# RWKV chunks: block-inverse matrices as 32x32 diagonal blocks, their products in 32x32 tiles

## The reference, cut to what matters

```
def wkv7_scan(r, w, k, v, a, b):
    def step(state, inp):
        r_t, w_t, k_t, v_t, a_t, b_t = inp
        sa = jnp.einsum('bhvk,bhk->bhv', state, a_t)
        state = state * w_t[:, :, None, :] + sa[..., None] * b_t[:, :, None, :] + v_t[..., None] * k_t[:, :, None, :]
        y_t = jnp.einsum('bhvk,bhk->bhv', state, r_t)
        return state, y_t
...
    g = jax.nn.sigmoid(xg @ g1) @ g2          # g1: 1024 x 160, g2: 160 x 1024
...
    y = wkv7_scan(r_h, decay, k_h, v_h, -kk, kk * a_h)   # 16 heads of 64
...
    return (y * g) @ w_o
```

## Time and profile before

| what | us |
|---|---|
| median of 3 runs (1687.45, 1694.29, 1691.63) | 1691.63 |
| the profiled execution, whole | 1687.7 |
| its span, first to last instruction | 1685.9 |
| PE busy in it | 1653.5 |
| stage of the change: chunks, 1368.2 to 1462.7 | 94.5 |
| gate, first part (L1190, L1192), from 1331.8 | 7.1 |
| gate, second part (L1207, L1208), from 1361.2 | 7.0 |

### The profile page before, as it was taken

One profiled execution on the slowest core, in us unless ns is written; L12 is line 12 of the kernel. 1 busy time (PEld: TensorE's weight loads), 2 busy tenths in 40 slices (PEclk: granted clock), 3 DMA queues, 4 the chain that ended last, 5 costly groups with the idle time before them and its releaser, 6 DMA issues.

```text
span 1685.9 us, 32004 instructions
## 1 busy us (share of the span) xinstructions
PE 1653.5 (98%) x11846; PEld 1456.5 (86%) x11846; DVE 1081.1 (64%) x1979; ACT 947.3 (56%) x1416; POOL 1126.6 (67%) x505
## 2 busy tenths in 40 slices
PE   8999999999999999999999999999999999999998
PEld 6888889999999999888888769888888899888887
DVE  5324242997546766679999986455557975855555
ACT  5458553445544444566555667565667942356555
POOL 6964776788788898776676438656476551846463
PEclk9999999999999999999999999999999999999999
DMA  8544444566655455689999945555543412155551
GB/s 309 197 150 145 155 150 175 163 193 194 187 169 169 154 170 156 189 306 366 377 374 403 411 182 176 199 201 190 184 162 121 168 27 78 53 197 181 197 187 74
DMA packets 95998, 330.35 MB, mean 196 GB/s; under 512 B 32896, under 2 KB 33424, under 8 KB 78368
## 3 DMA queue, kind: packets, MB, share of 16 engines
q1 hardware_dynamic: 84448, 295.32, 51.3%
q0 software_dynamic: 11312, 33.68, 5.2%
q10 hardware_dynamic: 144, 0.07, 0.0%
HBM read 322.73 MB, written 5.24 MB: 195 GB/s over the span
## 4 chain that ended last, share of the span: by engine, by line
PE 74%; POOL 10%; issue 6%; DVE 4%; DMA 3%; ACT 3%; POOLq 0%; DVEq 0%; SPq 0%; ACTq 0%
PE bank L1088 8%; POOL rows_lo L3096 7%; PE bank L893 7%; PE bank L1109 6%; PE bank L968 5%; PE bank L899 4%; PE bank L1092 4%; PE bank L636 4%; PE bank L642 4%; PE bank L637 4%; PE bank L1224 3%; PE bank L925 3%; PE bank L959 2%; PE bank L963 2%; PE bank L965 2%
## 5 line engine op out<-in xcount | busy, mean ns | idle before, releaser
L3081 POOL TENSOR_TENSOR unit_lo<-unit_raw,unit_hi 128x2048 fp32r<-128x2048 f32 (+1 forms) x86 | 336.1, 3926 | 145.2 <-ACT unit_hi L1697 118.9
L3096 POOL TENSOR_TENSOR rows_lo<-rows_raw,rows_hi 128x1024 fp32r<-128x1024 f32 x128 | 309.2, 2417 | 73.1 <-ACT rows_hi L1817 46.0
L3171 POOL TENSOR_TENSOR up_lo<-up_raw,up_hi 128x2048 fp32r<-128x2048 f32 x22 | 111.3, 5057 | 156.6 <-ACT up_hi L1977 127.0
L1895 ACT ACTIVATE rows_hi<-rows_raw 128x1024 fp32r<-128x1024 f32 x128 | 135.8, 1061 | 118.1 <-PE bank L968 111.3
L2657 DVE TENSOR_TENSOR rows_lo<-rows_raw,rows_hi 128x1024 fp32r<-128x1024 f32 x128 | 160.3, 1256 | 23.3 <-ACT rows_hi L1895 23.0
L1697 ACT ACTIVATE unit_hi<-unit_raw 128x2048 fp32r<-128x2048 f32 x70 | 134.0, 1919 | 65.5 <-PE bank L642 36.8
L1088 PE MATMUL bank<-x_lo_hi,up_hi 128*128 128x512 f32 x640 | 159.8, 392 | 0.1
L899 PE MATMUL bank<-x_lo_hi,rows_lo 128*128 128x256 f32 x1024 | 143.3, 283 | 0.5 <-POOL rows_lo L3096 0.5
L899 PEld LDWEIGHTS bank<-x_lo_hi,rows_lo 128*128 128x128 f32 x1024 | 135.7, 190 | 6.4 <-POOL rows_lo L3096 0.9
L3134 POOL DMA_INDIRECT gathered<-in_v,picked_row x64 | 91.7, 1433 | 71.2 <-DVE bank L2647 61.5
L1088 PEld LDWEIGHTS bank<-x_lo_hi,up_hi 128*128 128x128 f32 x640 | 116.2, 189 | 21.9 <-issue 0.3
(11 more groups left out here) (511 smaller groups left out, 4186.3 us busy)
## 6 DMA issues: line engine op xcount, KB each, us to landing
unit_raw<-in_ring SPq DMA_DIRECT2D x70, 1024.0 KB, 4.9
rows_raw<-in_u SPq DMA_DIRECT2D x128, 512.0 KB, 3.6
rows_raw<-in_v SPq DMA_DIRECT2D x128, 512.0 KB, 7.2
up_raw<-in_up SPq DMA_DIRECT2D x44, 1024.0 KB, 5.0
down_raw<-in_down SPq DMA_DIRECT2D x22, 1024.0 KB, 5.0
unit_raw<-in_ring SPq DMA_DIRECT2D x20, 256.0 KB, 3.6
kept_hidden<-table SPq DMA_DIRECT2D x16, 256.0 KB, 4.1
const<-in_const SPq DMA_DIRECT2D x1, 1792.0 KB, 14.2
```

The costliest lines, as they stand in the source:

```text
L1895: A(rows_hi[q % 2][:, :], rows_raw[q][:, :], ACT.Copy).then_inc(S("v_hi_ready"), 1)
L3081: return nc.gpsimd.tensor_tensor(unit_lo[SLOT_OF[n]][:, w], unit_raw[SLOT_OF[n]][:, w], hi, ALU.subtract)
L3096: nc.gpsimd.tensor_tensor(rows_lo[q][:, :], rows_raw[q][:, :], rows_hi_f[q % 2], ALU.subtract).then_inc(S("u_lo_ready"), 1)
L3171: nc.gpsimd.tensor_tensor(whole(up_lo[l][s][1]), whole(up_raw[l][s][1]), as_f32(up_hi[s][1]), ALU.subtract).then_inc(S("up_lo1_ready"), 1)
```

## The change

The matrices of the inverse are block diagonal at 32 for most of the steps. They are now kept as their four 32x32 diagonal blocks (two heads of two blocks) in 256 columns in place of 512, and a product of two such matrices is a `block_products`: for each of the eight pairs four matmuls of 32x32 by 32x32, in four tiles of the array. That is 32 calls in place of 16. Eight products per chunk take this form (`x2`, `x4`, `r2`, `y8`, `r3`, `r4`, `mT`, `w`). The last two (`nT`, `tt`), which fill the lower left corner, have two tiles and 16 calls as before.

- DVE: the turns and sums of these matrices have 256 columns; a new add packs the masked matrix (`m_xd`), `corners` copies the corner blocks into `m_inv`.
- ACT: the copies have 256 columns; for the last chunk two activations write the diagonal blocks of `m_inv`.
- POOL: `first_sum` and `across_split` have 256 columns, `halves_placed` (512 columns) writes the diagonal blocks of `m_inv` for the first three chunks; six small steps at its start.
- Gate: the odd ranks are made in two column tiles of 128 tokens each (16 calls of 128 columns in place of 8 of 256); in the second part 16 calls of 128 columns for the first 128 ranks and 16 calls for the odd ranks with 32 rows each, at partitions 0 and 64, in place of 8 and 8 of 256 columns. `GATE2` is loaded by three DMAs in place of one.
- The stage begins when `rT` is scaled; `kfT` and the copy `dec_end` follow. SP waits for `halves_placed` before it loads `WO`.

```diff
+            def block_products(name, lhs, rhs, tiles=((0, 0), (1, 1), (2, 2), (3, 3))):
+
+                o = fill(name, len(tiles))
+                ends = [None] * len(tiles)
+                for p in range(PAIRS):
+                    for i, (k, m) in enumerate(tiles):
+                        ends[i] = mm(o[quarter(m), p * BLK:(p + 1) * BLK], lhs(quarter(k), p), rhs(quarter(k), p), start=True, stop=True)
+                full_by_heads(name, ends)
...
             def fourths(c, e):
                 made(c, "x2")
                 wait_turned("x2", c)
-                products(("x4", c), by_pair(m_y2[e]), by_pair(m_x2[e]))
+                block_products(("x4", c), by_pair(m_y2[e]), by_pair(m_x2[e]))
                 pe.wait_ge(S("r1_ready"), c + 1)
-                products(("r2", c), by_pair(m_y2[e]), inv_of(c))
+                block_products(("r2", c), by_pair(m_y2[e]), by_pair(m_iv[e]))
...
             def within_64(c, e):
                 wait_turned("q32", c)
-                products(("nT", c), by_pair(m_ex[e]), by_pair(m_x2[e]))
+                block_products(("nT", c), corner_of(e), by_pair(m_x2[e]), ((0, 1), (2, 3)))
...
             for k in range(KT):
-                t = mm(o[0:32, SEQ:2 * SEQ], g1[:, k * 160 + 128:(k + 1) * 160], mx_gate[:, k, :], start=k == 0, stop=k == KT - 1)
+                for c in range(TC):
+                    ends[c] = mm(o[last_ranks(c), SEQ:SEQ + P], g1[:, k * 160 + 128:(k + 1) * 160], mx_gate[:, k, c * P:(c + 1) * P], start=k == 0, stop=k == KT - 1)
...
-            for b in range(4):
-                o = fill(("g2", b))
-                for m in range(2):
-                    at_ = (2 * b + m) * P
-                    mm(o[:, m * SEQ:(m + 1) * SEQ], g2[:, at_:at_ + P], lora[:, 2, :], start=True, stop=False)
-                    t = mm(o[:, m * SEQ:(m + 1) * SEQ], g2[:, 1024 + at_:1024 + at_ + P], lora[:, 3, :], start=False, stop=True)
+            for b in range(2):
+                outs = [fill(("g2", c, b)) for c in range(TC)]
+                for m in range(4):
+                    at_ = (4 * b + m) * P
+                    for c in range(TC):
+                        mm(outs[c][:, m * P:(m + 1) * P], g2[:, at_:at_ + P], lora[:, 2, c * P:(c + 1) * P], start=m == 0, stop=False, skip_group_check=True)
+                for m in range(4):
+                    at_ = 1024 + (4 * b + m) * P
+                    for c in range(TC):
+                        r = last_ranks(c)
+                        t = mm(outs[c][:, m * P:(m + 1) * P], g2[r, at_:at_ + P], lora[r, 3, 0:P], start=False, stop=m == 3, skip_group_check=True)
...
+            def halves_placed(c):
+
+                wait_drained(g, ("w", c))
+                both = m_inv[c][:, :, :].rearrange("p m (n v) -> p m n v", n=2)
+                TT(both, bc(m_iv[c % 3][:, :, :].unsqueeze(2), [PAIRS, 2, BLK]), bc(own_half[:, :, :].unsqueeze(1), [PAIRS, 2, BLK]), ALU.mult).then_inc(S("halves_placed"), 1)
...
             for c in first:
                 x_of_chunk(c)
+            pe.wait_ge(S("chunks_ready"), 2)
             by_token(0)
-            for c in first:
+            squares(0, 0)
+            by_token(1)
+            for c in first[1:]:
                 squares(c, c)
-            by_token(1)
```

More of the change, by code:

```diff
@@ L426, in wait_loaded @@
         same = [m for m in range(n + 1) if SLOT_OF[m] == SLOT_OF[n]]
[L427 removed]
+        eng.wait_ge(raw_loaded[SLOT_OF[n]], 16 * sum(2 if m in (UNIT_AT["LORA1"], UNIT_AT["LORA2"]) else 3 if m == UNIT_AT["GATE2"] else 4 if m >= UNIT_AT["WO"] else 1 for m in same))
     def wait_released(eng, n):
@@ L2113, in _ @@
                 t = A(bonusT[:, m, :], bonusT[:, m, :], ACT.Copy, scale=col("r_k", m))
-            t.then_inc(S("bonus_scaled"), 1)
-            for b in range(4):
-                copy(("g2", b), gT[:, 2 * b:2 * b + 2, :])
+            t.then_inc(S("scaled_columns"), 1)
+            for b in range(2):
+                for c in range(TC):
+                    o = wait_filled(act, ("g2", c, b))
+                    drain(("g2", c, b), A(gT[:, 4 * b:4 * b + 4, c * P:(c + 1) * P], o[:, :].rearrange("p (m t) -> p m t", m=4), ACT.Copy))
             first = range(3)
@@ L2167, in _ @@
             rows_deviation(0)
-            copies(last, "nT", of(m_x4))
+            wait_drained(act, ("w", NRC - 1))
+            for n in range(2):
+                t = A(m_inv[NRC - 1][:, :, BLK * n:BLK * n + BLK], m_iv[lane(NRC - 1)][:, :, :], ACT.Copy, scale=own_half[:, n, 0:1])
+                step.mark(t) if n == 0 else t.then_inc(S("halves_placed"), 1)
+            block_copies(last, "nT", m_x4)
             wait_filled(act, ("ds", 1))
@@ L2964, in summed, with corners @@
                     wait_drained(ve, (after, c))
-                r = m_inv[c][:, :, :]
-                drain((name, c), V.tensor_tensor(r, eight(o), r, ALU.add))
+                r = m_iv[lane(c)][:, :, :]
+                drain((name, c), V.tensor_tensor(r, of_blocks(o), r, ALU.add))
+            def corners(c):
+                o = of_blocks(wait_filled(ve, ("tt", c)))
+                ve.wait_ge(S("halves_placed"), c + 1)
+                for par in range(2):
+                    r = quarter(2 * par)
+                    t = V.tensor_copy(m_inv[c][r, :, BLK:DK], o[r, :, :])
+                    step.mark(t) if par == 0 else drain(("tt", c), t)
             ve.wait_ge(S("compact_ready"), len(compact))
@@ L3034, in yg_lo_of @@
                     drain(("yt", th, b), V.tensor_tensor(yg_lo[w], o, yg_hi[w].bitcast(F32), ALU.subtract))
-            for b in range(4):
-                wait_drained(ve, ("g2", b))
+            for b in range(2):
+                for half in range(TC):
+                    wait_drained(ve, ("g2", half, b))
             o = eight(wait_filled(ve, ("y_", c)))
@@ L3211, in _ @@
                 step(nc.gpsimd.memset(eu16_c[DK * par:DK * par + half, half:DK], 0.0))
+            step(TT(ident_c[:, 0:BLK], ident_c[:, 0:BLK], ident_c[:, BLK:DK], ALU.add))
+            step(nc.gpsimd.memset(own_half[:, :, :], 0.0))
+            for n in range(4):
+                step(nc.gpsimd.memset(own_half[quarter(n), n % 2, :], 1.0))
             step(nc.gpsimd.memset(starts[:, :], 1.0))
@@ L3260, in _ @@
                 across_split(c)
+            for c in range(NRC - 1):
+                halves_placed(c)
             for c in (1, 2):
```

142 lines of the change are left out of this document (82 added, 60 removed).

## The result

The changed kernel takes **1718.62 us** (median of 5 runs, 1715.47 to 1720.3) against 1691.63 (median of 5 runs beside it, 1687.45 to 1696.07): ratio 1.0157, 95% interval 1.0142 to 1.0172. It is slower by 27.0 us, inside the predicted range and 8.6 us above the predicted 1710.

The account below looks back on a forecast made before the run. PE was taken to be bound by instruction arrival, about 3.75 us per 256. 18.3 + 5.5 - 3.2 - 1.0 = +19.6 us on a mean of 1690.3 gave 1710; own range 1700 to 1720, 8-in-10 range 1690 to 1726.

Parts of the forecast that it names:

- The first step: Dense part: PE already works at about the rate its instructions arrive, about 3.75 us per 256, as a limit, not a coincidence.
- First three chunks: Chunk stage's first part: 1536 more records, 16.0 blocks at 3.75 us, 61.3 us in all, an increase of 18.3 us.
- The 1.3 us for wide products at the start: Start of the chunks: three `x` products stand together and outlast their instructions' arrival; 1.3 us of 2.4 added.
- Bonus sums and first product of the last chunk: The stretch between the third chunk and the last chunk's later products; no change was forecast, 0.
- the rival of the fallen clock: Chunk stage: PE waiting for instructions with four small tiles looks idle, so the granted clock falls as well; 1722, chance 0.12.
- Last chunk: 1418.02 to 1442.70: 512 more records, 7.5 blocks, 30.2 us, so +5.5 us; the rest of the stage 0.
- The gate: Odd ranks in two tiles: -1.75 us in the first part, -1.65 in the second; -3.2 taken, bounds -3.4 and 0.
- The savings on DVE: Chunk stage: turns and sums of 256 columns take about half, some 20 us of DVE, worth 0 in time now.
- After the stage: Small waits that a later PE no longer meets, above all 0.86 us for POOL's `unit_lo`: -1.0 us.
- The cost per matmul: Rival for the products: 29 ns per record or a little less, not the fetch; 1704 to 1717, chance 0.10.
- the array sets the pace: Rival: instructions can arrive sooner, so a 32x32 product takes 0.47 to 0.6 us and the kernel is faster; 1679, chance 0.13.
- the half-plus-fixed cost: Rival: a call costs half of now plus a fixed part, about 33 ns, 1.05 us a product; 1690, chance 0.08.

Follow-up runs that it names:

- 64 columns a call: The changed kernel with 64 in place of 32 moving columns in every 32x32 matmul of the inverse, each block multiplied twice; 1718.75 us.
- shared weights: The changed kernel with `x4` and `r2`, which have the same stationary matrix, made by one set of 32 calls of 64 columns; 1712.44 us.
- bfloat16, 32x32: The changed kernel with the inverse's 32x32 matrices kept in bfloat16, at lower precision, so half the instructions per call; 1684.24 us.
- bfloat16, shared weights: The changed kernel with the inverse's matrices in bfloat16 and `x4` and `r2` made by one set of calls; 1682.33 us.
- bfloat16, 64x64: The kernel before with the gate's edit, 64x64 tiles, inverse and solve products in bfloat16, one DVE copy more per chunk; 1680.19 us.

## Why the prediction was right, and where its sizes were off

**The first step held as a limit, not as the reason for the 58 ns.** The prediction staked itself on this: that PE was already at the rate at which instructions arrive, and that this was no coincidence. More instructions do run into a limit: a product with double the instructions takes half a block of 3.97 us, so 1.99 us, in the dense part in place of 0.93. But what set the 0.93 us before was the 64x64 product's own time on PE, for it takes 0.98 us in the changed kernel where its instructions are there (1377.73 to 1378.71 above), and the kernel before has no stop at a block border in its first three chunks. That this time and the arrival rate are nearly the same was a coincidence, which let two readings agree on 1.87 us. The first three chunks of each kernel, with the records (MATMUL and LDWEIGHTS) of the rows above divided by 256:

| kernel | records | blocks | us | us a block |
|---|---|---|---|---|
| before | 2562 | 10.0 | 42.96 | 4.29 |
| after | 4099 | 16.0 | 64.45 | 4.03 |
| 64 columns a call | 4100 | 16.0 | 64.56 | 4.03 |
| shared weights | 3714 | 14.5 | 57.84 | 3.99 |
| bfloat16, 32x32 | 2372 | 9.3 | 36.25 | 3.91 |
| bfloat16, shared weights | 2179 | 8.5 | 34.84 | 4.09 |
| bfloat16, 64x64 | 1604 | 6.3 | 33.66 | 5.37 |

Tile shape, data type, columns and clock differ, and the time is 3.9 to 4.1 us a block in every kernel that stops at the borders. In the kernel before, PE is busy for 42.58 of 42.96 us and the wide products add to it; in the last row DVE sets the pace in part.

The block of 256 is what the counts show: 127 MATMUL and 127 LDWEIGHTS records from stop to stop, one or two more on the border, and 9 packets more on q8 for 2144 PE records more, 238 a packet (72 and 63 packets; 12918 and 11846 records of each of the two kinds). An instruction of 64 bytes is the prediction's assumption, the one size at which 256 of them fill the 16 KB; no run shows it by itself. PE stops for 1.8 to 2.5 us at eight borders in a row between 1384.8 and 1412.4. That the next block is asked for only when PE enters the one before agrees with the packets here, each of which begins 0.8 to 1.7 us after a restart. How many instructions can wait ahead of PE no run here shows; its first stop comes at 1380.3, 652 records after the start of the chunks.

**First three chunks: +21.5, not +18.3. This is the first of two terms that failed: it was mis-sized.** I took "about 3.75 us a block", the quiet spacing of packets; that spacing was the pace at which PE worked off its 64x64 products, not the fastest or the usual delivery. From the restart at 1380.84 to the end of the part, 13.5 blocks take 53.41 us, 3.97 us each. 16 x 0.22 is 3.5 us, and the difference is 3.2. The forecast had the better number in hand: 1.4 us from restart to packet and 2.6 from there to its use, 4.0 us. I read these as a value under traffic, though the row shows the queues idle. What remains open is why a block could follow each 3.7 us where PE never stopped. In the last chunk, too, two blocks take 7.34 us together (1452.56 to 1459.90), with a stop at only one of their borders, so 3.97 us is the usual time of a block and not a hard floor. The 1.3 us for wide products at the start come out near 0.9: 64.45 less 16 x 3.97.

**Bonus sums and first product of the last chunk: +3.5, not 0.** This term was put at nothing, and it is the second that failed: here the rival of the fallen clock came true in part. The granted clock is at the lower level (0.50) from 1385.0 to 1415.7 and again from 1432.8 to 1446.5; each time it fell within 0.4 us of the restart after a stop, of 2.46 and 1.48 us. In the dense part this is free, as the experiment with 64 columns shows (mean clock 0.92 and 64.56 us, against 0.75 and 64.45). The bonus sums are not short of instructions, though, and pay in full: the sums start at 1434.25 and the wide product at 1441.17 in the changed kernel, 6.9 us, where they were 3.7 apart. The wide product behind them adds only 0.2, since it was at the lower clock before too (0.55 on the mean from 1414.80 to 1418.02). The rival's 1722, 12 us above the forecast, was an estimate that no run shows; in its place stand the 3.5 us of this part. It was too high because 64x64 products at the lower clock can lie under the waits for instructions: in the last chunk four of them take 1.7 to 1.8 us each at a mean clock of 0.50 to 0.58 (from 1453.51 and 1460.15), where they took 0.93, and the two blocks that hold the first pair still take only 7.34 us.

```profile
1434.25 6.99 PE L1337 MATMUL bank<-const,bonusT 128*128 128x2 f32 x32
1441.17 3.68 PE L1245 MATMUL bank<-r_k_a,aaT 64*64 64x128 f32 x32
```

**Last chunk: +3.8 and +0.9, predicted +5.5 and 0.** Together 4.6 for 5.5. 1922 records (7.5 blocks) took 28.44 us, 3.8 a block; the estimate of 30.2 gave too much to the traffic. This part begins after 10 us in which PE needed few instructions, so some may have been there already, which would make its mean lower than 3.97; no run tests this.

**The gate: -2.6, not -3.2**, inside the bounds of -3.4 and 0. The odd ranks of the first part halve as forecast, those of the second fall less. In the timeline of the changed kernel the first part's 32 records take 1.9 us where there were 3.5, and 16 of the second part's take 1.1, so 2.2 for 32 where 3.5 became 1.8 in the forecast:

```profile
1339.57 1.94 PE L1212 MATMUL bank<-mx_gate,unit_raw 128*32 128x128 f32 x32
...
1363.76 1.95 PE L1228 MATMUL bank<-lora,unit_raw 128*128 128x128 f32 x16
1365.64 1.16 PE L1233 MATMUL bank<-lora,unit_raw 32*128 32x128 f32 x16
```

In the second part a record of 128 columns beside 128x128 weights costs 0.12 us (1363.76 to 1365.64, 16 records) and not the 0.11 taken, so the halved calls with the first ranks are not quite free: 3.8 us for 32 where 3.5 was forecast.

**The savings on DVE: 0, as said.** DVE is busy for 5.1 us less in the first part and 11.5 us less in the kernel, and none of it is seen in the time. In the stage it is 8.2 us (60.10 to 51.95), not the forecast 20: sums and turns of 256 columns take 0.42 and 0.45 us (0.65 and 0.71 before), which is more than half, and new steps came in:

```profile
L3014 DVE TENSOR_TENSOR m_iv<-bank,m_iv x12: 386/424/425, 1386.3 to 1425.9; 128x256 f32<-128x256 f32 x12
L3004 DVE STREAM_TRANSPOSE m_x<-m_iv x6: 445/446/446, 1409.6 to 1426.3; 128x256 f32<-128x256 f32 x6
```

**After the stage: -0.6, predicted -1.0.** The reason given for this term did not hold: PE still waits 0.82 us for POOL's `unit_lo` (0.86 before), and its other waits in the first 30 us behind the stage are the same. What the 0.6 us are, no run shows.

**The other rivals.** The cost per matmul fell with the stops and the 0.68 us of a product of 64 records, 10.6 ns each (the 25 ns a record at which the expectation for bfloat16 begins is shown by no row or run; the records there are 12 ns apart); "the array sets the pace" was right that the array becomes faster (0.68 us a product) and wrong that it sets the pace; the half-plus-fixed cost of 1.05 us a product is neither the 0.68 us with instructions at hand nor the 2 us in practice.

**How near the number was, and why.** The measured 1718.62 is 8.7 us above the sum of 1709.9: 3.2 from the first three chunks, 3.5 from the clock, 0.6 from the gate and 0.4 from the rest, less 0.9 in the last chunk, then 1.3 because the sum was added to 1690.3 and not to the median, and 0.6 that the parts leave over. It lies nearer to the fallen clock's 1722 than to 1710. The mechanism, delivery by blocks, is what the runs show; that the number stayed inside its range owes something to luck, since the size of a block's time was read from a kernel that never waited for one. The forecast's own range was also worked out too narrow: with 23.5 blocks, 3.5 us a block moves the sum by -5.9, not -4, and the 3.97 measured lies above its 3.9.

## What to carry to other kernels

Count the instructions of a stretch before its array time: in this kernel 256 PE instructions that made 3.7 us of work ran without stops, and those that made 2 us of work took 3.97. There the stretch is bound by their delivery, and a product split into twice the calls cost double (1.99 us for 0.93), whatever the array gained (0.68). A float32 call is four such instructions, so packing (two products with the same weights in one wider call, larger tiles, one pass) is worth more there than a faster pass: shared weights gave 6.2 us here, while the faster 32x32 pass, in twice the calls, lost 29.7. The signs are stops "for issue" with 127 and 127 records between them and no other engine at work; they were few in the kernel before, which just meets the limit (1.8 us in its stage, against 27.9 in the changed one). Two rates that happen to be equal do not tell which of them is the limit; a place where one of them is out of the way does (here, a 64x64 product right behind a fast one). Of the float32 versions tried here, the kernel before with the gate's edit alone is the fastest: 1688.93 us.

## What was not expected of the hardware

- A matmul record of a 32x32 float32 product takes 10.6 ns on the mean (0.68 us for 64), and one of a 64x64 bfloat16 product 15.6 ns (0.25 us for 16). A record of a 64x64 float32 product takes 29 ns (0.93 us for 32); both of the others are well below it.
- The granted clock falls to its lower level, 0.50, at 1385.0, just after the first long stop of the dense part (2.46 us), and stays there while PE works 1.9 us on 32x32 products and stands still 2 us in turn. It comes back at 1415.7, in a wide product, after 3.3 us without a stop. With 64 columns a call in the same places the mean clock of the part is 0.92 in place of 0.75.
- The few stops of up to 1.17 us in the last chunk of the kernel before vanish when the loads of `WO` are held back, but also, with the loads in place, when only the gate is changed. What makes an instruction packet late there is open.
